# The RMS norms of a hybrid decoder layer: the roots of the rows enter TensorE's turning products as a diagonal matrix

## The chip, the cores and the metric

The kernel runs on one core of one Trainium2 chip. The metric is the device time of one execution in microseconds (us). A profile of one execution lies beside it; its times are counted from the start of its span.

## The reference

One layer of a decoder trunk, float32, 512 tokens behind 16 learned meta tokens, width 2048:

```
def rms_norm(x, g):
    y = x * rsqrt(mean(x * x, axis=-1) + 1e-6)
    return y * g

h = concat(meta_tokens, x)                       # 528 x 2048
proj = rms_norm(h, ln_mix_g) @ w_in              # 528 x 5632
h = h + concat(attention(proj), hgrn2(proj)) @ w_out
h = h[16:]                                       # 512 x 2048
h = h + peer_ffn(rms_norm(h, ln_ffn_g), ...)     # routing, 16384 experts, top 16 of 8 heads
```

Both norms over the width, the one ahead of the input projection and the one ahead of the routing, are what the change touches. The norms over single heads are other code.

## The kernel before, in words

`build` (L2054) calls the stages in order: `norm_rows` for the first norm ("mixnorm", L2150), `project`, `attend`, `recur`, `mix_out`, `norm_rows` for the second norm ("ffnnorm", L2157), `route`, `gate_table`, `experts`. Each stage is a block with a program for each engine, and the engines meet at its end. Nothing is planned by costs: the order on each engine is the order of the code.

`norm_rows` (L112) has the rows in four tiles of 128 tokens by 2048 columns, and in the first norm also 16 meta rows. What follows needs them turned (columns on the partitions), multiplied by a gain that belongs to the column, and split into a high part of type float32r and a low part (the remainder), since products are made of three float32r products (`product`, L341).

- ScalarE (ACT) sums the squares in the first norm (L163), except for one tile that VectorE (DVE) sums (L195); in the second norm the sums come from `mix_out`. ACT takes the square root (L167), then makes the high parts of the first two weight pieces of the next stage (`split_first_high`, L300).
- DVE takes the reciprocal with one correction step (`inverse_root`, L100). It then multiplies each tile by its roots, 128x2048 at a time (L206): in place in the first norm, into the tensor `scaled_rows` in the second. The meta rows follow (L209). Each multiplication raises the semaphore `scaled`.
- TensorE (PE) turns: `turn(tb, c)` (L229) is a transpose of 128 columns c of tile tb, out of the scaled tile with the identity `c_ident` as the other operand, into one of 6 PSUM banks (`NORM_BANKS`); a bank holds column block c of all four tiles. It does columns 0 to 5 of tile 0, then of tiles 1, 2 and 3, waiting for `scaled` before each tile. Then it turns the meta rows (L242, 16 transposes). Then for columns 6 to 15 it waits until the bank is emptied (`low`) and does the four tiles.
- ACT empties each bank into the high part with the gain (L171). DVE then makes the low part out of the same bank (L212) and so frees it. Behind the last column the meta rows are treated likewise (L217, L175, L221).
- GpSimd (POOL) makes the low parts of the two first weight pieces (`split_first_low`, L306, which is L312). In the first norm it narrows a mask ahead of that. In the second it makes `plain_rows` behind that (`plain`, L2137): tile 3 of `scaled_rows` multiplied by the gain as a row, which SyncE (SP) stores (L2135) for the sparse experts. SP waits for POOL there (`plain_ready`); the routing's DVE waits for the store (`plain_stored`, L1569).

Behind the first norm PE begins `project` (L343 to L345, with `w_in`), behind the second `route` (the same lines, with `w_q`; the scores of a head, L1425, are float32 products with the keys, not split).

Of the kernel before, what the change touches and what calls it, by code (L numbers as in the profile page):

```python
# [24 lines left out]
ALU = mybir.AluOpType  # L25
ACT = mybir.ActivationFunctionType
AX = mybir.AxisListType
F32 = mybir.dt.float32
# [4 lines left out]
P = 128  # L33
D = 2048
DC = D // P
T = 512
TB = T // P
M = 16
# [73 lines left out]
def norm_rows(nc, tag, tiles, scaled_tiles, meta, gain, parts, columns, ident, place, kb, stream,  # L112
# [11 lines left out]
    with ExitStack() as ctx:  # L124
        def sem(name):
# [5 lines left out]
        scaled, turned, high, low = sem("scaled"), sem("turned"), sem("high"), sem("low")  # L131
# [3 lines left out]
        stat = place(f"{tag}_stat", [P, 4, 8], F32, kb)  # L135
        squares = [place(f"{tag}_squares{i}", [P, D], F32, kb + 1 + 8 * i) for i in range(2)] \
            if sums is None else []
        meta_whole = place(f"{tag}_meta_whole", [P, DC, M], F32, kb + 17) if meta is not None else None
# [38 lines left out]
        @block.gpsimd  # L177
        def _(pool):
            if pool_first:
                pool_first(pool)  # L180
            stream.split_first_low(pool)
            if pool_last:
                pool_last(pool, scaled)

        @block.vector
        def _(dve):
# [18 lines left out]
            for tb in range(TB):  # L205
                dve.tensor_scalar(scaled_tiles[tb], tiles[tb], stat[:, 3, tb:tb + 1], None, ALU.mult)\  # L206
                    .then_inc(scaled, 1)
            if meta is not None:
                dve.tensor_scalar(meta, meta, stat[0:M, 3, TB:TB + 1], None, ALU.mult).then_inc(scaled, 1)  # L209
# [14 lines left out]
        @block.tensor  # L224
        def _(pe):
            if consts:
                pe.wait_ge(*consts)

            def turn(tb, c):  # L229
                return pe.transpose(banks[c % NORM_BANKS][:, tb, :], scaled_tiles[tb][:, c * P:(c + 1) * P],  # L230
                                    ident[:, :])

            for tb in range(TB):
                pe.wait_ge(scaled, tb + 1)
                for c in range(NORM_BANKS):
                    last = turn(tb, c)
                    if tb == TB - 1:
                        last.then_inc(turned, 1)
            if meta is not None:
                pe.wait_ge(scaled, n)  # L240
                for c in range(DC):
                    last = pe.transpose(meta_bank[:, c, :], meta[:, c * P:(c + 1) * P], ident[0:M, 0:M])  # L242
                last.then_inc(meta_turned, 1)
            for c in range(NORM_BANKS, DC):
                pe.wait_ge(low, c - NORM_BANKS + 1)
                for tb in range(TB):
                    last = turn(tb, c)
                last.then_inc(turned, 1)
# [5 lines left out]
NORM_BANKS = 6  # L254
# [1799 lines left out]
def build(nc, a, out):  # L2054
# [16 lines left out]
    scaled_rows = place("scaled_rows", [P, TB, D], F32, 144)  # L2071
# [20 lines left out]
                                          ("gain_row_in", "plain_ready", "plain_stored"))  # L2092

# [43 lines left out]
    def plain(pool, scaled):  # L2137
        pool.wait_ge(gain_in, 16)
        pool.wait_ge(scaled, TB)
        pool.tensor_tensor(plain_rows[:], scaled_rows[:, TB - 1, :], gain_row[:], ALU.mult).then_inc(plain_ready, 1)  # L2140

    def load_rows(sp, loaded):
        load_early(sp)
        sp.dma_start(meta_rows[:, :], a["meta"]).then_inc(loaded[0], 16)
        for tb in range(TB):
# [4 lines left out]
    spent = norm_rows(nc, "mixnorm", rows, rows, meta_rows[:, :], cst["ln_mix"], hn,  # L2150
                      lambda part, c: part[:, c, M:L].rearrange("p (b t) -> p b t", t=P), cst["ident"],
                      place, 138, w_in, load_rows, (early_in, 16 * len(early)), pool_first=narrow_mask)
# [4 lines left out]
    norm_rows(nc, "ffnnorm", [h[:, tb, :] for tb in range(TB)], [scaled_rows[:, tb, :] for tb in range(TB)],  # L2157
              None, cst["ln_ffn"], xT, lambda part, c: part[:, :, c, :], cst["ident"], place, 136, w_q,
# [78 lines left out]
```

## Time and profile before

| | |
|---|---|
| time, median of 3 runs | 3590.52 us (3590.32 to 3590.65) |
| the profiled execution, its own time | 3590.52 us |
| its span | 3588.7 us |
| PE busy | 3360.4 us (94%) |
| DVE busy | 2234.7 us (62%) |
| ACT busy | 1124.8 us (31%) |
| POOL busy | 1158.9 us (32%) |
| first norm's turning and splitting, from DVE's first scaling to the projection's first product | 19.25 to 38.37 us |
| the same in the second norm, to the routing's first product | 1048.20 to 1069.83 us |

The busy times are sums over the span and overlap each other. PE is TensorE's matmuls, PEld its weight loads. The timeline gives instructions in order of time, merged where they follow each other; in brackets stands how long the engine had been idle and what ended it. Time beyond the span is what lies around the program.

### The profile page before, as it was taken

What the parts mean: (1) busy time and instruction counts of PE and PEld (TensorE: products, weight loads), DVE (VectorE), ACT (ScalarE), POOL (GpSimd) and SP (SyncE); (2) the same over time, 40 slices, a digit from 0 to 9 for tenths busy, and PEclk for the clock granted to TensorE, in tenths of its full rate; (3) what the DMA queues carried; (4) which work ended last, traced back from release to release, by engine and by line L of the source; (5) the groups of instructions that cost most, each with busy time, mean ns of one, the idle gap of its engine ahead of it and who ended that gap; (6) DMA issues with size and microseconds to landing.
All of it is one profiled execution on the core that took longest, in us unless ns stands there. A gap on an engine that the chain in (4) does not pass through costs nothing.

```text
span 3588.7 us, 51464 instructions
## 1 busy us (share of the span) xinstructions
PE 3360.4 (94%) x16926; PEld 2943.4 (82%) x16926; DVE 2234.7 (62%) x3867; ACT 1124.8 (31%) x1743; POOL 1158.9 (32%) x870
## 2 busy tenths in 40 slices
PE   7999999677989957899999999999999999999999
PEld 5778876566868746799899899999998998998998
DVE  2003312695026989677777777767777777777776
ACT  3122223443222239523322222232223233222222
POOL 2344431163435520232332322323333333333322
PEclk9999999798999979999999999999999999999999
DMA  4233320002332204888788888877888887888886
GB/s 139 76 88 94 94 82 15 1 1 101 99 105 83 71 35 187 293 270 267 260 272 265 266 267 267 269 265 261 275 262 265 268 266 261 270 265 265 268 266 232
DMA packets 276020, 686.84 MB, mean 191 GB/s; under 512 B 120544, under 2 KB 120800, under 8 KB 273504
## 3 DMA queue, kind: packets, MB, share of 16 engines
q1 hardware_dynamic: 202224, 417.51, 36.0%
q0 software_dynamic: 73728, 268.47, 22.2%
q8 instruction: 37, 0.61, 0.1%
q14 instruction: 31, 0.25, 0.0%
HBM read 655.48 MB, written 30.41 MB: 191 GB/s over the span
## 4 chain that ended last, share of the span: by engine, by line
PE 59%; ACT 2%; issue 1%; DMA 1%; DVE 0%; ACTq 0%; DVEq 0%; SPq 0%
PE exp_a L1866 10%; PE exp_a L1868 10%; PE exp_a L1867 10%; PE exp_o L1887 10%; PE exp_o L1889 10%; PE exp_o L1885 10%; ACT table_gaps L1684 1%; ACT table_stage L1700 1%; DMA gate_table<-table_stage 0%; PE table_b L1644 0%; DMA exp_raw<-in_v 0%; DVE table_hot L1670 0%; ACTq L1684 0%; ACTq L1700 0%; PE table_t L1635 0%
## 5 line engine op out<-in xcount | busy, mean ns | idle before, releaser
L1866 PE MATMUL exp_a<-x_high,exp_uh 128*128 128x384 f32 x2048 | 685.9, 335 | 11.6 <-DVE exp_ul L1950 11.6
L1868 PE MATMUL exp_a<-x_high,exp_ul 128*128 128x384 f32 x2048 | 685.7, 335 | 0.0
L1867 PE MATMUL exp_a<-x_low,exp_uh 128*128 128x384 f32 x2048 | 685.4, 335 | 0.0
L1889 PE MATMUL exp_o<-exp_vh,exp_al 128*128 128x512 f32 x1536 | 598.2, 389 | 0.0
L1887 PE MATMUL exp_o<-exp_vl,exp_ah 128*128 128x512 f32 x1536 | 598.1, 389 | 0.0
L1885 PE MATMUL exp_o<-exp_vh,exp_ah 128*128 128x512 f32 x1536 | 597.5, 389 | 0.0
L1845 POOL DMA_INDIRECT exp_rows<-in_v_rows,exp_now x256 | 323.6, 1264 | 712.2 <-DVE h L1971 653.7
L1845 POOL DMA_INDIRECT exp_rows<-in_u_rows,exp_now x256 | 298.7, 1167 | 734.2 <-DVE exp_rows L1964 689.2
L1915 ACT CAST exp_vh<-exp_raw 128x1024 fp32r<-128x1024 f32 x256 | 260.1, 1051 | 516.7 <-PE exp_o L1889 493.3
L1950 DVE TENSOR_TENSOR exp_vl<-exp_raw,exp_vh 128x1024 fp32r<-128x1024 f32 x256 | 304.6, 1220 | 166.6 <-ACT exp_vh L1915 165.5
L1866 PEld LDWEIGHTS exp_a<-x_high,exp_uh 128*128 128x128 f32 x2048 | 385.6, 188 | 13.2 <-DVE exp_ul L1950 7.5
L1867 PEld LDWEIGHTS exp_a<-x_low,exp_uh 128*128 128x128 f32 x2048 | 385.5, 188 | 1.2
L1868 PEld LDWEIGHTS exp_a<-x_high,exp_ul 128*128 128x128 f32 x2048 | 385.3, 188 | 0.0
L1926 ACT ACTIVATE exp_act<-exp_a 128x384 f32<-128x384 f32 x128 | 63.0, 492 | 962.5 <-PE exp_a L1868 793.4
L1889 PEld LDWEIGHTS exp_o<-exp_vh,exp_al 128*128 128x128 f32 x1536 | 288.3, 188 | 60.0
L1887 PEld LDWEIGHTS exp_o<-exp_vl,exp_ah 128*128 128x128 f32 x1536 | 288.3, 188 | 59.3
L1885 PEld LDWEIGHTS exp_o<-exp_vh,exp_ah 128*128 128x128 f32 x1536 | 288.3, 188 | 59.2
L1950 DVE TENSOR_TENSOR exp_ul<-exp_raw,exp_uh 128x1024 fp32r<-128x1024 f32 x256 | 309.7, 1221 | 42.0 <-ACT exp_uh L1915 31.6
L312 POOL TENSOR_TENSOR w_in_lo<-w_in_raw,w_in_hi 128x1024 fp32r<-128x1024 f32 x88 | 212.8, 2418 | 333.1 <-ACT w_in_hi L298 333.0
L1971 DVE SCALAR_TENSOR_TENSOR h<-exp_rows,exp_weights,h 128x1024 f32<-128x1024 f32 x256 | 316.5, 1277 | 0.0
L1964 DVE SCALAR_TENSOR_TENSOR exp_rows<-exp_rows,sparse_x 128x1024 f32<-128x1024 f32 x256 | 302.3, 1217 | 0.0
L1991 DVE TENSOR_TENSOR exp_act<-exp_act,exp_gates 128x384 f32<-128x384 f32 x128 | 71.9, 562 | 358.8 <-ACT exp_act L1926 291.5
(292 smaller groups left out, 5194.7 us busy)
## 6 DMA issues: line engine op xcount, KB each, us to landing
exp_raw<-in_u SPq DMA_DIRECT2D x256, 512.0 KB
exp_raw<-in_v SPq DMA_DIRECT2D x256, 512.0 KB
w_in_raw<-in_w_in SPq DMA_DIRECT2D x88, 512.0 KB, 3.6
gate_table<-table_stage SPq DMA_DIRECT2D x6, 4096.0 KB, 11.6
exp_gates<-gate_table SPq DMA_DIRECT2D x128, 192.0 KB
w_out_raw<-in_w_out SPq DMA_DIRECT2D x32, 512.0 KB, 3.6
w_q_raw<-in_w_q SPq DMA_DIRECT2D x32, 512.0 KB, 3.8
x_rows<-in_x SPq DMA_DIRECT2D x4, 1024.0 KB, 8.1
```

Of the source, the lines that this page charges most:

```text
L312: eng.tensor_tensor(self.lo[:, g % 2], self.raw[:, g % RAW], self.hi[:, g % 2].bitcast(F32), ALU.subtract).then_inc(self.low, 1)
L1845: pool.indirect_dma_start(rows[slot][:, :], None, sparse["u" if kind == "dot" else "v"], bass.IndirectOffsetOnAxis(ap=now[:, turn, place_n ...
L1866: pe.matmul(bank, uh[:, b, c, :], xh[:, 0:DENSE_TB, c, :], start=(c == 0), stop=False)
L1867: pe.matmul(bank, uh[:, b, c, :], xl[:, 0:DENSE_TB, c, :], start=False, stop=False)
L1868: last = pe.matmul(bank, ul[:, b, c, :], xh[:, 0:DENSE_TB, c, :], start=False, stop=(c == DC - 1))
L1885: pe.matmul(bank[:, :], ah[:, key, tokens], vh[:, dc % 2, key, :], start=(key == 0), stop=False)
L1887: pe.matmul(bank[:, :], ah[:, key, tokens], vl[:, dc % 2, key, :], start=False, stop=False)
L1889: last = pe.matmul(bank[:, :], al[:, key, tokens], vh[:, dc % 2, key, :], start=False, stop=(key == KEYS_OF_MACRO - 1))
L1915: act.copy(part(uh if split[0] == "u" else vh, *split, half), raw[:, c % RAW_SLOTS, :])\
L1950: dve.tensor_tensor(part(ul if kind == "u" else vl, kind, which, half), raw[:, slot, :], part(uh if kind == "u" else vh, kind, which, half ...
L1964: done = dve.scalar_tensor_tensor(rows[slot][:, :], rows[slot][:, :], 1.0, sparse["x"][:, half, :], ALU.mult, ALU.mult, accum_out=dots[:, ...
L1971: done = dve.scalar_tensor_tensor(sums, rows[slot][:, :], weights[:, pl(pick(m, kind, t), 1)], sums, ALU.mult, ALU.add)
```

## The change

Tiles are no longer multiplied by their roots. DVE instead multiplies the identity by each tile's roots, which gives a 128x128 diagonal matrix (`scales`, one for each tile, and `meta_scale`, 16x16), and PE's transposes become float32 matmuls of the tile with that matrix. `plain`, which had the scaled tile, multiplies tile 3 by its roots on POOL itself, waits for that, and multiplies by the gain row. The tensor `scaled_rows` goes.

```diff
             for tb in range(TB):
-                dve.tensor_scalar(scaled_tiles[tb], tiles[tb], stat[:, 3, tb:tb + 1], None, ALU.mult)\
+                dve.tensor_scalar(scales[:, tb, :], ident[:, :], stat[:, 3, tb:tb + 1], None, ALU.mult)\
                     .then_inc(scaled, 1)
             if meta is not None:
-                dve.tensor_scalar(meta, meta, stat[0:M, 3, TB:TB + 1], None, ALU.mult).then_inc(scaled, 1)
+                dve.tensor_scalar(meta_scale[:, :], ident[0:M, 0:M], stat[0:M, 3, TB:TB + 1], None, ALU.mult)\
+                    .then_inc(scaled, 1)
...
             def turn(tb, c):
-                return pe.transpose(banks[c % NORM_BANKS][:, tb, :], scaled_tiles[tb][:, c * P:(c + 1) * P],
-                                    ident[:, :])
+                return pe.matmul(banks[c % NORM_BANKS][:, tb, :], tiles[tb][:, c * P:(c + 1) * P],
+                                 scales[:, tb, :], start=True, stop=True)
...
                 for c in range(DC):
-                    last = pe.transpose(meta_bank[:, c, :], meta[:, c * P:(c + 1) * P], ident[0:M, 0:M])
+                    last = pe.matmul(meta_bank[:, c, :], meta[:, c * P:(c + 1) * P], meta_scale[:, :],
+                                     start=True, stop=True)
...
-    def plain(pool, scaled):
+    def plain(pool, scaled, roots):
         pool.wait_ge(gain_in, 16)
         pool.wait_ge(scaled, TB)
-        pool.tensor_tensor(plain_rows[:], scaled_rows[:, TB - 1, :], gain_row[:], ALU.mult).then_inc(plain_ready, 1)
+        pool.tensor_scalar(plain_rows[:], h[:, TB - 1, :], roots[:, TB - 1:TB], None, ALU.mult)\
+            .then_inc(plain_scaled, 1)
+        pool.wait_ge(plain_scaled, 1)
+        pool.tensor_tensor(plain_rows[:], plain_rows[:], gain_row[:], ALU.mult).then_inc(plain_ready, 1)
```

## Rows read from the trace of the kernel before

**Rows 1.** The page: busy time, share of the span and instructions of each engine.

```profile
PE 3360.4 (94%) x16926; PEld 2943.4 (82%) x16926; DVE 2234.7 (62%) x3867; ACT 1124.8 (31%) x1743; POOL 1158.9 (32%) x870
```

**Rows 2.** Timeline, first norm: start us, duration us, engine, line, operation [idle before].

```profile
19.25 4.87 DVE L206 TENSOR_SCALAR x_rows<-x_rows,mixnorm_stat 128x2048 f32<-128x2048 f32 x4
...
20.68 4.86 PE L230 MATMUL mixnorm_bank<-c_ident,x_rows 128*128 128x128 f32 x24 [20.68 <-DVE x_rows L206]
...
25.00 9.35 ACT L171 ACTIVATE hn_high<-mixnorm_bank,c_ln_mix 128x512 fp32r<-128x512 f32 x16 [4.94 <-PE mixnorm_bank L230]
25.47 1.07 PEld L242 LDWEIGHTS mixnorm_meta_bank<-c_ident,meta_rows 16*128 16x128 f32 x16 [0.17 <-DVE meta_rows L209]
...
25.72 10.62 DVE L212 SCALAR_TENSOR_TENSOR hn_low<-mixnorm_bank,c_ln_mix,hn_high 128x512 fp32r<-128x512 f32 x16 [0.42 <-ACT hn_high L171]
...
27.18 0.42 PEld L230 LDWEIGHTS mixnorm_bank<-c_ident,x_rows 128*128 128x128 f32 x4 [0.20 <-DVE hn_low L212]
...
38.37 0.79 PE L343 MATMUL proj_bank<-w_in_hi,hn_high 128*128 128x512 f32 x1 [5.27 <-DVEq L484]
```

**Rows 3.** Timeline, second norm, with the same columns.

```profile
1048.17 5.63 POOL L312 TENSOR_TENSOR w_q_lo<-w_q_raw,w_q_hi 128x1024 fp32r<-128x1024 f32 x2 [11.44 <-ACT w_q_hi L304]
1048.20 9.08 DVE L206 TENSOR_SCALAR scaled_rows<-h,ffnnorm_stat 128x2048 f32<-128x2048 f32 x4
...
1051.65 1.54 PE L230 MATMUL ffnnorm_bank<-c_ident,scaled_rows 128*128 128x128 f32 x6 [7.60 <-DVE scaled_rows L206]
...
1057.43 4.55 POOL L2140 TENSOR_TENSOR plain_rows<-scaled_rows,ln_ffn_row 128x2048 f32<-128x2048 f32 x1 [3.62 <-DVE scaled_rows L206]
1058.01 9.36 ACT L171 ACTIVATE x_high<-ffnnorm_bank,c_ln_ffn 128x512 fp32r<-128x512 f32 x16 [8.97 <-PE ffnnorm_bank L230]
1058.73 10.62 DVE L212 SCALAR_TENSOR_TENSOR x_low<-ffnnorm_bank,c_ln_ffn,x_high 128x512 fp32r<-128x512 f32 x16 [1.46 <-ACT x_high L171]
...
1069.83 0.77 PE L343 MATMUL route_q<-x_high,w_q_hi 128*128 128x512 f32 x1 [3.71 <-PEq L124]
```

**Rows 4.** One line's instructions, L206 and L312: duration ns min/median/max, starts us.

```profile
L206 DVE TENSOR_SCALAR x_rows<-x_rows,mixnorm_stat x4: 1280/1281/1286, 19.2 to 22.8; 128x2048 f32<-128x2048 f32 x4
...
L206 DVE TENSOR_SCALAR scaled_rows<-h,ffnnorm_stat x1: 3395/3395/3395, 1048.2 to 1048.2; 128x2048 f32<-128x2048 f32 x1
L312 POOL TENSOR_TENSOR w_q_lo<-w_q_raw,w_q_hi x1: 3327/3327/3327, 1050.5 to 1050.5; 128x1024 fp32r<-128x1024 f32 x1
```

**Rows 5.** Groups by line, gate table, DVE: busy us, mean ns | idle.

```profile
L1670 DVE TENSOR_SCALAR table_hot<-c_iota,picksT 128x128 f32<-128x128 f32 x384 | 103.0, 336 | 0.0
```

**Rows 6.** Float32 products: routing scores, recurrence (timeline), gate table at half clock.

```profile
L1425 PEld LDWEIGHTS route_s<-sub_keys,route_qT x16: 187/192/192, 1098.3 to 1100.1; 128*128 128x128 f32 x16
L1425 PE MATMUL route_s<-sub_keys,route_qT x16: 270/275/275, 1098.5 to 1100.2; 128*128 128x128 f32 x16
...
706.04 1.16 PE L1103 MATMUL rec_g<-rec_halves 128*128 128x128 f32 x8 [1.24 <-DVE rec_halves L1171]
...
L1644 PEld LDWEIGHTS table_b<-table_hot x5: 288/333/338, 1322.1 to 1323.0; 128*128 128x128 f32 x5
```

**Rows 7.** Windows: busy us of each engine, PEclk (granted clock), DMA share, GB/s.

```profile
35.00:36.00 1.00, 0.00 (x0) 0.00 (x0) 1.00 (x3) 0.00 (x0) 0.00 (x0) 0.57 0.00 0
...
41.50:42.00 0.50, 0.50 (x3) 0.38 (x2) 0.00 (x0) 0.00 (x0) 0.00 (x0) 0.54 1.01 410
...
1048.00:1049.00 1.00, 0.00 (x0) 0.00 (x0) 0.96 (x2) 1.00 (x2) 0.83 (x1) 0.95 0.99 418
...
1069.00:1069.80 0.80, 0.00 (x0) 0.00 (x1) 0.36 (x1) 0.00 (x0) 0.00 (x0) 0.73 0.00 0
...
1072.50:1073.00 0.50, 0.50 (x3) 0.43 (x2) 0.00 (x0) 0.00 (x0) 0.00 (x0) 0.71 0.98 385
...
1325.00:1326.00 1.00, 1.00 (x9) 1.00 (x8) 1.00 (x4) 0.15 (x1) 0.00 (x0) 0.81 0.95 348
```

**Rows 8.** Timeline, attention: weight loads of score products with 16 and 256 columns.

```profile
646.36 1.18 PEld L835 LDWEIGHTS att_s<-att_kT,att_qT 128*128 128x128 f32 x8
```

More of the change, by code:

```diff
@@ L106, in inverse_root, with norm_rows @@
     link(dve.tensor_tensor(out, out, spare, ALU.mult))
-def norm_rows(nc, tag, tiles, scaled_tiles, meta, gain, parts, columns, ident, place, kb, stream,
+def norm_rows(nc, tag, tiles, meta, gain, parts, columns, ident, place, kb, scales_kb, stream,
               loads, consts=None, sums=None, pool_first=None, pool_last=None):
@@ L137, in norm_rows @@
             if sums is None else []
+        scales = place(f"{tag}_scales", [P, TB, P], F32, scales_kb)
+        meta_scale = place(f"{tag}_meta_scale", [M, M], F32, kb + 0.25) if meta is not None else None
         meta_whole = place(f"{tag}_meta_whole", [P, DC, M], F32, kb + 17) if meta is not None else None
@@ L182, in _ @@
             if pool_last:
-                pool_last(pool, scaled)
+                pool_last(pool, scaled, stat[:, 3, :])
         @block.vector
@@ L2070, in build @@
     plain_rows = place("plain_rows", [P, D], F32, 185)
-    scaled_rows = place("scaled_rows", [P, TB, D], F32, 144)
     plain_table = nc.dram_tensor("plain_rows_table", [P, D], F32, kind="Internal").ap()
@@ L2092, in build @@
                                           ("gain_row_in", "plain_ready", "plain_stored"))
+    plain_scaled = nc.alloc_semaphore("plain_scaled")
     cst, kb = {}, 193.0
@@ L2149, in build @@
     rows = [x_rows[:, tb, :] for tb in range(TB)]
-    spent = norm_rows(nc, "mixnorm", rows, rows, meta_rows[:, :], cst["ln_mix"], hn,
+    spent = norm_rows(nc, "mixnorm", rows, meta_rows[:, :], cst["ln_mix"], hn,
                       lambda part, c: part[:, c, M:L].rearrange("p (b t) -> p b t", t=P), cst["ident"],
-                      place, 138, w_in, load_rows, (early_in, 16 * len(early)), pool_first=narrow_mask)
+                      place, 138, 164, w_in, load_rows, (early_in, 16 * len(early)), pool_first=narrow_mask)
     spent = project(nc, place, 176.5, w_in, hn, nat, nat_meta, meta_row, turned, cst, spent)
@@ L2156, in build @@
     mix_out(nc, place, w_out, mix, mixT, h, a["x"], cst, sums, w_q.load_start)
-    norm_rows(nc, "ffnnorm", [h[:, tb, :] for tb in range(TB)], [scaled_rows[:, tb, :] for tb in range(TB)],
-              None, cst["ln_ffn"], xT, lambda part, c: part[:, :, c, :], cst["ident"], place, 136, w_q,
+    norm_rows(nc, "ffnnorm", [h[:, tb, :] for tb in range(TB)], None, cst["ln_ffn"], xT, lambda part, c: part[:, :, c, :], cst["ident"], place, 136, 144, w_q,
               load_keys, sums=sums, pool_last=plain)
```

## The prediction

> **What bounds the kernel now.** I read the page's busy times first, then the stretches around the two calls of `norm_rows` in the timeline, then the clock by windows. TensorE is busy for 94% of the span [rows 1], nearly all of it outside the norms, so what counts is by how much a norm delays the product stage behind it. The reader should see in each norm three phases. First VectorE scales four tiles of rows and TensorE turns the first six columns of each tile. Then ACT and DVE empty a bank each 0.66 us (10.62 us for 16 [rows 2, 3]), with TensorE turning the other ten columns beside them: four transposes take 0.42 us of weight loads [rows 2], so TensorE waits there and DVE sets the pace. Last comes a tail: 2.0 us in the first norm from DVE's last full-width low part (25.72 + 10.62 = 36.34) to TensorE's first product (38.37), and 0.5 us in the second (69.35 to 69.83; I leave off the leading thousand for the second norm from here on). Any shift of that first product is passed on whole, because the stages behind it are TensorE's.
>
> **The scaling that goes.** In the first norm it is 4.87 us of DVE [rows 2], but PE is busy with the 24 first transposes in nearly the same time, 4.86 us from 20.68: only the first tile's 1.28 us lies alone on the path [rows 4]. In the second it is 9.08 us [rows 3], because DVE and POOL exclude each other: the first scaling lasts 3.40 us where one of the first norm is 1.28, and POOL's second split 3.33 of the 5.63 that both take, where the first was 2.3 [rows 3, 4]. POOL's first ran 48.17 to 50.5, DVE's scaling only behind it, POOL's second behind that. The Trainium skill ("SBUF — State Buffer", Who interferes with whom) says that whoever issues first holds the shared ports for its whole instruction and the other blocks fully; the trace agrees with it, with these durations.
>
> **What comes in its place on DVE.** A multiplication of a 128x128 tile. The nearest row is a TENSOR_SCALAR of 128x128 with two operations, 0.336 us [rows 5]. I take 0.30 for one operation; no other value between nothing and 0.34 moves the sum by more than 0.3 us a norm. First norm: the first diagonal is ready at 19.25 + 0.30. PE starts 1.43 after DVE's start today, 0.15 after the 1.28 of a scaling, and so at 19.70 then, 0.98 us earlier. The other four diagonals, the meta rows' among them, need 1.2 us together and never gate PE. Second norm: the first diagonal is asked for at 48.20, waits for POOL until 50.3, is ready at 50.6, and PE starts at 50.75 (51.65 today). The second diagonal probably waits for POOL's second split (50.5 to 52.9) and is ready at 53.2; PE needs until 53.4 for the first tile's six products at 0.44, which hides it. The third and fourth follow by 53.9.
>
> **What comes on TensorE.** This is the main term. A transpose of float32 is one weight load and one matmul; a float32 product of 128x128 is two of each: the routing scores of one head are 8 products and the trace counts 16 [rows 6]. The pieces start (1100.2 - 1098.5)/15 = 0.113 us apart at the full clock there, 0.112 from here on; eight in 1.16 us in the recurrence, less the last one's 0.275, are 0.126. At half clock they start (1323.0 - 1322.1)/4 = 0.22 apart [rows 6]. So a column of four products costs PE 8 x 0.112 = 0.90 us where four transposes were out in 0.42. It passes DVE's 0.66: **the second phase becomes TensorE's**.
>
> **The first norm, step by step.** The clock is at half when PE starts: the first 24 transposes take 4.86 us, 0.20 each, twice what they take later, although the record of the clock has no event there. It rose 3.3 us after PE's start in the table stage, 3.6 in the projection, 3.0 in the routing [rows 2, 3, 6, 7]; I take 3.3. From 19.70 to 23.0 PE issues 15 of the first 48 pieces at 0.22; the other 33 at 0.112 take it to 26.7. Bank 0 is complete with piece 38, at 25.6 + 0.3 = 25.9, so ACT starts 0.9 us later than today's 25.00. The meta rows' 16 transposes took 1.07 us [rows 2]; they become 32 pieces with 16 moving columns. The nearest row is the attention's eight score pieces, four of them with 16 columns and four with 256: their loads start (1.18 - 0.19)/7 = 0.14 apart on average [rows 6, 8], and with 0.22 for the wide ones (twice the columns of 0.112) the narrow are 0.085 or less. So 2.7 us, to 29.4; ends: 0.067, as for the transposes, and 0.112, as for full pieces, 2.1 to 3.6 us. Ten columns at 0.90 end at 38.4. Behind the last come 0.2 of matmul latency, ACT's 0.72 (25.00 to 25.72) and DVE's 0.66 with 0.1 for its semaphore: 40.1 for 36.34: **3.7 us later**. With the bounds (meta pieces, 0.112 or 0.126 a piece, clock 3.0 or 3.6 after the start) it is 3.0 to 6.0.
>
> **The second norm.** PE from 50.75, clock up at 54.05 after 15 pieces, 48 pieces out at 57.75, bank 0 at 56.95 (58.01 today). The seventh column needs DVE's first low part, at 56.95 + 1.5 = 58.45; ten columns end at 67.5, the last low part at 69.2 for 69.35: **0.15 us earlier**, between 1.0 earlier and 1.5 later. The gain ahead of the first bank, 1.1 us, is given back by the slower second phase.
>
> **POOL and SP.** `plain` now starts with a multiplication of 128x2048. POOL has no such row; its two-operand multiplication of that size is 4.55 us [rows 3], the upper end. From 53.9 it then ends at 58.4 at the latest and the second at 63.0 (62.0 today), ahead of 69.2, so I cost it and SP's store behind it at nothing. The cover is 6 us; if it went, the barrier at the block's end would wait for POOL.
>
> **The clock behind the norms.** The second norm ends today with PE idle for 3.71 us; the clock fell 0.5 us before the routing's first product and was back at 72.8, 3.0 us after it [rows 3, 7]: 7 products at 0.43 where 0.23 would do, 1.4 us. Now PE idles only from 67.6 to 69.7. The clock fell 2.0, 3.1 and 4.9 us after PE stopped (idle of 5.27, 3.71 and 7.60 us [rows 2, 3], the fall in each by rows 7), so at 2.0 to 2.1 us it most likely stays: **1.4 us earlier**. Behind the first norm PE idles from 38.5 to 42.1, 3.6 us instead of 5.3, and two of the three falls came sooner: I take no gain there, with 1.5 us as the other end.
>
> **Sum.** 3.7 - 0.15 - 1.4 = +2.2 us. The profiled execution took 3590.52 us with a span of 3588.7, 1.8 us around it, and its time is the median of the three runs. Span 3590.9, time **3592.7 us**. That is 0.06%, below the 0.2% (7.2 us) that I count as distinguishable.
>
> **The rivals.**
> 1. *Products keep the clock up where transposes didn't.* The clock in this trace rose during transposes too, so they count for something, but it fell soonest (2.0 us) behind a stretch of them. Then the projection starts at full clock (1.5 us less) and the first pieces are sooner fast (0.3 us): 3590.9. The Trainium skill ("TensorE: Matmul & The Clock Gate", Part 4: PE-mode transpose) says that transpose mode doesn't count as PE-busy in the same way and full clock doesn't engage for it; taken strictly this trace contradicts it, in degree it would favour this rival. Chance 0.25.
> 2. *The small multiplications don't exclude POOL.* Then the second norm's PE starts at 48.6, everything up to the tenth column comes 2 us sooner: 3590.7. For it: nothing in the rows has this size beside POOL; against: the same operation with 2048 columns was blocked. Chance 0.12.
> 3. *A product costs what a transpose costs.* Then DVE's pace stays; the first norm gains 1.0 us and the second 3: 3586.5. The doubled count of the routing scores speaks against it. Chance 0.03. That the scaling isn't removed at all can't be: the calls pass the unscaled tiles.
> 4. *Slower: the clock doesn't rise in the norms, or falls again between bank waits.* PE's second phase then costs 10 x 8 x 0.22 = 17.6 us for 9.0, in both norms: 8.6 us each, 3609.9; in one of them alone, 3601.3. It decides from the point where the clock is at half as column 6 starts (29.4 and 58.5). Against it: PE is denser than today and today the clock is full there. Chance 0.04.
>
> **How the numbers follow.** The forecast has 0.56 and is the likeliest. Its bounds and rivals 1 and 2 reach from 3589 to 3597; what lies outside is rivals 3, 4 and a mishap, some 0.1. Faster by over 0.2% is under 3583.3: 0.01. Slower by over 0.2% is above 3597.7: rival 4 and the upper tail of the piece price, 0.05. Between: 0.94.
>
> **What would show it.** L206 in the changed profile: eight instructions of 128x128 near 0.3 us, two of them in the second norm long because of POOL. L230: twice the count, and in the second phase PE without idle, DVE's L212 waiting for ACT and ACT for PE, 0.9 us a column. ACT's first in the first norm at 25.9, the projection's first product at 42.1, the routing's at 69.7 plus the 3.7 us of the first norm, with full clock there and half at the projection. Wrong would be: L230's count unchanged, DVE still at 0.66 a column, or the products half as dense.

## The result and the profile after

The changed kernel takes 3599.05 us (median of 13 runs, 3594.34 to 3603.4) where the kernel before takes 3590.52 (median of 13, 3585.89 to 3595.69). The ratio is 1.0022 with a 95% interval of 1.0014 to 1.0031: **slower by 7.9 us** (5.0 to 11.1), outside the stated range of 3589 to 3597. (An execution of this kernel differs from the next by up to 9 us, so single times are weak evidence below, and stages are compared instead.) Its profiled execution took 3598.11 us with a span of 3596.3. TensorE gained instructions, 144 net, and 14.6 us of busy time; DVE lost 7.0 us of busy time [rows 1]:

```profile
PE 3375.0 (94%) x17070; PEld 2963.3 (82%) x17070; DVE 2227.7 (62%) x3867; ACT 1127.8 (31%) x1743; POOL 1165.5 (32%) x871
```

144 is 64 more pieces for each norm's tiles and 16 for the meta rows: each transpose became two.

| stage (from the two profiled executions, us) | before | after | shift |
|---|---|---|---|
| first norm, DVE's first multiplication | 19.25 | 19.22 | 0 |
| projection's first product | 38.37 | 45.97 | +7.6 |
| second norm, DVE's first multiplication | 1048.20 | 1054.97 | +6.8 |
| routing's first product | 1069.83 | 1077.33 | +7.5 |
| gate table's first transpose | 1316.50 | 1323.59 | +7.1 |
| end of the span | 3588.7 | 3596.3 | +7.6 |

All of it is there at the projection's first product. The timeline of the first norm in the changed kernel, with the columns of [rows 2]:

```profile
19.22 0.88 DVE L208 TENSOR_SCALAR mixnorm_scales<-c_ident,mixnorm_stat 128x128 f32<-128x128 f32 x4
19.66 8.32 PE L233 MATMUL mixnorm_bank<-mixnorm_scales,x_rows 128*128 128x128 f32 x48 [19.66 <-DVE mixnorm_scales L208]
26.90 3.57 ACT L173 ACTIVATE hn_high<-mixnorm_bank,c_ln_mix 128x512 fp32r<-128x512 f32 x6 [6.86 <-PE mixnorm_bank L233]
...
27.62 4.04 DVE L215 SCALAR_TENSOR_TENSOR hn_low<-mixnorm_bank,c_ln_mix,hn_high 128x512 fp32r<-128x512 f32 x6 [7.39 <-ACT hn_high L173]
27.91 3.74 PE L245 MATMUL mixnorm_meta_bank<-mixnorm_meta_scale,meta_rows 16*128 16x16 f32 x32
...
31.58 10.82 PE L233 MATMUL mixnorm_bank<-mixnorm_scales,x_rows 128*128 128x128 f32 x80
...
34.86 0.69 ACT L173 ACTIVATE hn_high<-mixnorm_bank,c_ln_mix 128x512 fp32r<-128x512 f32 x1 [1.02 <-PE mixnorm_bank L233]
...
38.87 0.69 ACT L173 ACTIVATE hn_high<-mixnorm_bank,c_ln_mix 128x512 fp32r<-128x512 f32 x1 [0.21 <-PE mixnorm_bank L233]
...
45.97 0.79 PE L347 MATMUL proj_bank<-w_in_hi,hn_high 128*128 128x512 f32 x1 [3.57 <-DVEq L488]
```

Before, ACT and DVE each went through sixteen banks in one merged row without a pause [rows 2]. Now they stop after six, and ACT waits for TensorE ahead of each of the other ten: 2.69 us ahead of the first of them, behind the meta pieces, up to 1.02 in the slow stretch, and 0.21 where the clock is full. TensorE has no pause from 19.66 to 42.40 (31.58 + 10.82): the second phase is its own. Yet 80 pieces take 10.82 us there and 9.20 in the second norm, and the windows say why (busy time of PE, PEld, DVE, ACT, POOL, then the granted clock, the DMA share and GB/s):

```profile
31.00:32.00 1.00, 1.00 (x9) 0.97 (x9) 0.66 (x2) 0.00 (x0) 1.00 (x1) 1.00 0.09 16
32.00:33.00 1.00, 1.00 (x8) 1.00 (x7) 0.00 (x0) 0.00 (x0) 0.29 (x1) 0.60 0.00 0
33.00:34.00 1.00, 1.00 (x7) 1.00 (x7) 0.12 (x1) 0.69 (x1) 0.00 (x0) 0.50 0.00 0
34.00:35.00 1.00, 1.00 (x6) 1.00 (x6) 0.63 (x1) 0.14 (x1) 0.00 (x0) 0.50 0.00 0
35.00:36.00 1.00, 1.00 (x9) 1.00 (x8) 0.42 (x1) 0.55 (x1) 0.00 (x0) 0.70 0.00 0
```

PE is busy for the whole of every microsecond, and still the granted clock goes from full (2.4 GHz) to half (1.2 GHz) at about 32.2 and comes back at about 35.6. What TensorE had issued just before the fall are the 32 pieces of the meta rows.

The second norm, timeline, with the columns of [rows 3]:

```profile
1054.95 4.65 POOL L316 TENSOR_TENSOR w_q_lo<-w_q_raw,w_q_hi 128x1024 fp32r<-128x1024 f32 x2 [11.44 <-ACT w_q_hi L308]
1054.97 5.10 DVE L208 TENSOR_SCALAR ffnnorm_scales<-c_ident,ffnnorm_stat 128x128 f32<-128x128 f32 x4
1057.43 8.28 PE L233 MATMUL ffnnorm_bank<-ffnnorm_scales,h 128*128 128x128 f32 x48 [6.60 <-DVE ffnnorm_scales L208]
1060.27 5.44 POOL L2144 TENSOR_SCALAR plain_rows<-h,ffnnorm_stat 128x2048 f32<-128x2048 f32 x1 [0.67 <-DVE ffnnorm_scales L208]
...
1064.62 6.09 ACT L173 ACTIVATE x_high<-ffnnorm_bank,c_ln_ffn 128x512 fp32r<-128x512 f32 x10 [8.81 <-PE ffnnorm_bank L233]
...
1066.15 9.20 PE L233 MATMUL ffnnorm_bank<-ffnnorm_scales,h 128*128 128x128 f32 x80 [0.45 <-DVE x_low L215]
...
1077.33 0.47 PE L347 MATMUL route_q<-x_high,w_q_hi 128*128 128x512 f32 x1 [1.98 <-PEq L124]
```

And L208, one line's instructions (ns min/median/max):

```profile
L208 DVE TENSOR_SCALAR mixnorm_scales<-c_ident,mixnorm_stat x4: 280/280/287, 19.2 to 19.8; 128x128 f32<-128x128 f32 x4
L208 DVE TENSOR_SCALAR ffnnorm_scales<-c_ident,ffnnorm_stat x4: 274/1330/2400, 1055.0 to 1059.8; 128x128 f32<-128x128 f32 x4
```

The multiplication is 0.28 us by itself and 2.40 where POOL had issued first, so POOL's split keeps out the small multiplication too. The four together still take 5.10 us of DVE, but only the first gates TensorE. From DVE's first multiplication to the routing it was 21.63 us and is 22.36.

### The profile page after: what moved, and what is told of

Its sections match the earlier page's. It is cut to its first block, busy times and chain, and to the rows that moved or that the text cites. A ratio compares the mean times of both kernels' runs of the same rounds, so it can differ in the third digit from the quotient of the medians.

```text
span 3596.3 us, 51755 instructions
## 1 busy us (share of the span) xinstructions
PE 3375.0 (94%) x17070; PEld 2963.3 (82%) x17070; DVE 2227.7 (62%) x3867; ACT 1127.8 (31%) x1743; POOL 1165.5 (32%) x871
## 4 chain that ended last, share of the span: by engine, by line
PE 59%; ACT 2%; issue 1%; DMA 1%; ACTq 0%; DVE 0%; DVEq 0%; SPq 0%
PE exp_a L1870 10%; PE exp_a L1872 10%; PE exp_a L1871 10%; PE exp_o L1891 10%; PE exp_o L1893 10%; PE exp_o L1889 10%; ACT table_gaps L1688 1%; ACT table_stage L1704 1%; DMA gate_table<-table_stage 0%; PE table_b L1648 0%; DMA exp_raw<-in_v 0%; ACTq L1688 0%; ACTq L1704 0%; DVE table_hot L1674 0%; PE table_t L1639 0%
## 5 line engine op out<-in xcount | busy, mean ns | idle before, releaser
L1954 DVE TENSOR_TENSOR exp_ul<-exp_raw,exp_uh 128x1024 fp32r<-128x1024 f32 x256 | 309.7, 1220 | 41.9 <-ACT exp_uh L1919 31.6
```

The costliest lines, as they stand in the source:

```text
L1954: dve.tensor_tensor(part(ul if kind == "u" else vl, kind, which, half), raw[:, slot, :], part(uh if kind == "u" else vh, kind, which, half ...
```

## The experiments

### Which norm

The first two runs keep both forms in `norm_rows` and choose by call: products in one norm, scaled rows and transposes as before in the other.

```diff
             for tb in range(TB):
-                dve.tensor_scalar(scales[:, tb, :], ident[:, :], stat[:, 3, tb:tb + 1], None, ALU.mult)\
-                    .then_inc(scaled, 1)
+                dve.tensor_scalar(scales[:, tb, :] if products else scaled_tiles[tb],
+                                  ident[:, :] if products else tiles[tb],
+                                  stat[:, 3, tb:tb + 1], None, ALU.mult).then_inc(scaled, 1)
...
             def turn(tb, c):
+                if not products:
+                    return pe.transpose(banks[c % NORM_BANKS][:, tb, :], scaled_tiles[tb][:, c * P:(c + 1) * P],
+                                        ident[:, :])
```

**Products in the first norm alone.** 

> The change in the first norm alone; the second norm scales its rows and transposes as before. Theory: nearly all of the loss sits in the first norm. The projection's first product at 46.0 us (38.4 before), the stretch from DVE's first scaling to the routing's first product in the second norm 21.6 us as before (1048.20 to 1069.83), time 7.6 us over before. Rival: the loss is spread over later stages (a changed placement in time, not the norms): then the projection starts at 46.0 but the end moves by something else than 7 to 8 us.

Measured: 3598.4 us, ratio 1.0025 (1.0016 to 1.0035): 9.0 us, all of the loss. The timeline's first product of the projection, at 45.46 for 38.37, and the clock's fall in the windows, without a pause of PE:

```profile
45.46 0.79 PE L351 MATMUL proj_bank<-w_in_hi,hn_high 128*128 128x512 f32 x1 [3.57 <-DVEq L492]
```
```profile
31.00:32.00 1.00, 1.00 (x6) 0.97 (x6) 0.15 (x1) 0.00 (x0) 1.00 (x1) 0.55 0.00 0
```

**Products in the second norm alone.** 

> The change in the second norm alone. Theory: the stretch in the second norm is 0.7 us longer (22.4 us for 21.6), the routing then starts at full clock and gets 1.4 us back: 0.7 us faster than before, which no timing here separates from no change. Rival: the second norm costs as much as the first, 3 us or more.

Measured: ratio 1.0003 (0.9994 to 1.0012), no difference. The stretch is 22.40 us (1047.41 to 1069.81), and the routing runs at the full clock from its start.

```profile
1069.81 0.47 PE L349 MATMUL route_q<-x_high,w_q_hi 128*128 128x512 f32 x1 [1.98 <-PEq L124]
```

What follows: the loss is the first norm's, and the two parts (9.0 and 1.1 us by the middles of their intervals) add up to the whole (7.9) within these intervals. The 0.7 us of gain that was expected of the second norm lies inside its interval too.

### The meta rows and the clock

The first norm differs from the second by the meta rows' pieces, and there alone the clock fell. The six runs below change only them; the table also has the first norms of two runs that come further down. The first three columns of numbers are the durations of merged rows of PE's timeline; "to the projection" is counted from TensorE's first piece to the projection's first product, since DVE's start differs by some tenths (17.69 us in the kernel before). The last column is the time, with that of the kernel before from the same series; all but the first two are single executions. Until its first fall the record of the clock shows 1.00 in every trace, also where weight loads of 333 ns show the half clock, so rises in this norm are read from the weight loads.

| run | first 48 | meta pieces | last 80 | clock fell, was back | to the projection | time (before) |
|---|---|---|---|---|---|---|
| after | 8.32 | 3.74 | 10.82 | 32.2, 35.6 | 26.31 | 3599.05 (3590.52) |
| products in the first norm alone | 7.78 | 3.74 | 10.83 | 31.1, 34.5 | 25.77 | 3598.40 (3590.43) |
| after, POOL waits in the second norm | 8.02 | 3.74 | 10.82 | 31.6, 35.0 | 25.99 | 3589.86 (3586.43) |
| scaled rows and products | 7.08 | 4.36 | 11.79 | 30.4, 37.3 | 26.62 | 3599.99 (3586.43) |
| meta rows transposed (16) | 7.00 | 1.17 | 9.20 | not in the norm's pieces | 20.77 | 3594.99 (3590.43) |
| 16 rows, 128 columns | 6.93 | 4.69 | 11.55 | 29.3, 36.1 | 26.58 | 3598.82 (3590.43) |
| 128 rows, 16 columns | 7.27 | 3.90 | 10.56 | 30.1, 33.5 | 24.94 | 3603.05 (3586.43) |
| meta pieces first | 7.88 | 6.97 | 9.20 | rose only at 31 | 27.97 | 3597.24 (3586.43) |
| meta pieces last | 7.11 | 3.79 | 9.20 | 39.8, behind the 80 | 22.66 | 3595.58 (3589.50) |
| meta pieces spread | 7.94 | spread | spread | not in the norm's pieces | 26.93 | 3597.36 (3591.52) |

**Meta rows scaled and transposed as before**, the tiles turned by products:

```diff
-                    last = pe.matmul(meta_bank[:, c, :], meta[:, c * P:(c + 1) * P], meta_scale[:, :],
-                                     start=True, stop=True)
+                    last = pe.transpose(meta_bank[:, c, :], meta[:, c * P:(c + 1) * P], ident[0:M, 0:M])
```

> The changed kernel, but the 16 meta rows are scaled by their roots on DVE and turned by transposes as before. Theory: the meta rows' pieces cost 3.67 us for 1.1 and, beyond that, the TensorE clock falls behind them (0.60 at 32 to 33 us, half until 35.6), which costs 1.7 us in the last ten columns. Projection's first product at 46.0 - 2.6 - 1.7 = 41.7 us, and no half-clock stretch between the first 48 pieces and column 15. Rival (the clock falls at that time whatever is issued): the last ten columns still take 10.6 us, the projection starts at 43.4.

Measured: the projection at 40.65, 5.3 us sooner than in the changed kernel.

```profile
26.81 1.17 PE L244 MATMUL mixnorm_meta_bank<-c_ident,meta_rows 16*128 16x16 f32 x16
27.91 9.20 PE L232 MATMUL mixnorm_bank<-mixnorm_scales,x_rows 128*128 128x128 f32 x80
...
40.65 0.79 PE L345 MATMUL proj_bank<-w_in_hi,hn_high 128*128 128x512 f32 x1 [3.54 <-DVEq L486]
```
```profile
34.00:35.00 1.00, 1.00 (x11) 1.00 (x11) 0.85 (x2) 0.79 (x2) 0.00 (x0) 1.00 0.00 0
```

The clock holds, and all three terms shrink: the meta pieces by 2.6, the slow stretch by 1.6, and the first 48, which this run doesn't touch, by 1.3. So the last is the clock's own scatter. The projection behind it met that scatter too: by windows its clock was back at 46.7, 6.1 us after its first product, where the changed kernel's was back 3.3 us after. The 16 transposes are also over in 1.1 us; a stretch of transposes as long as 3.7 us wasn't tried, so this run says that the pieces of the meta products let the clock fall, not that transposes would have held it.

**Meta pieces with 128 moving columns** instead of 16, their rows still 16. The 16x16 diagonal becomes the first 16 rows of a 128x128 one, and the bank gets 112 columns more, which nothing reads:

```diff
-                    last = pe.matmul(meta_bank[:, c, :], meta[:, c * P:(c + 1) * P], meta_scale[:, :],
+                    last = pe.matmul(meta_bank[:, c * M:c * M + P], meta[:, c * P:(c + 1) * P], meta_scale[:, :],
```

> The changed kernel, but each product of the meta rows has 128 moving columns (16 of the diagonal, 112 zeros, which the next product overwrites) where it had 16; same number of pieces. Theory: the clock falls because pieces with 16 moving columns leave the array idle for most of their 0.112 us although the profile calls TensorE busy. With 128 columns the pieces come at the same 0.112 us, but the clock stays at full: the last ten columns in 9.0 us for 10.6, projection at 44.3. Rival 1 (a contraction over 16 rows, or zeros, is what doesn't count): clock falls as before, 46.0. Rival 2 (wide pieces are dearer): meta stretch over 4 us.

Measured: the clock fell all the same, sooner and for longer (29.3 to 36.1). The theory that narrow columns alone do it falls.

```profile
26.48 4.69 PE L246 MATMUL mixnorm_meta_bank<-mixnorm_meta_scale,meta_rows 16*128 16x128 f32 x32
31.10 11.55 PE L234 MATMUL mixnorm_bank<-mixnorm_scales,x_rows 128*128 128x128 f32 x80
```
```profile
29.00:30.00 1.00, 1.00 (x8) 1.00 (x8) 1.00 (x2) 0.05 (x1) 1.00 (x2) 0.63 0.00 0
```

**Meta pieces with 128 rows and 16 columns** (they read tile 0 and its diagonal, so the meta rows' values are replaced):

```diff
-                    last = pe.matmul(meta_bank[:, c, :], meta[:, c * P:(c + 1) * P], meta_scale[:, :],
+                    last = pe.matmul(meta_bank[:, c, :], tiles[0][:, c * P:(c + 1) * P], scales[:, 0, 0:M],
```

> The changed kernel, but the 32 narrow pieces take their weights from tile 0 of the token rows (128 rows) and 16 columns of its diagonal, instead of 16 rows: the meta rows' values are left out, tokens' values stand in their place. Same count, same 16 moving columns. Theory (what lets the clock fall is a product over 16 of the 128 rows): clock full through 27 to 36 us, last ten columns 9.0 us. Rival (few moving columns or diagonals nearly all zero also let it fall): clock falls 3 to 4 us after the pieces begin, last ten columns over 10 us.

```profile
26.83 3.90 PE L245 MATMUL mixnorm_meta_bank<-mixnorm_scales,x_rows 128*128 128x16 f32 x32
30.56 10.56 PE L233 MATMUL mixnorm_bank<-mixnorm_scales,x_rows 128*128 128x128 f32 x80
```
```profile
30.00:31.00 1.00, 1.00 (x7) 1.00 (x7) 0.68 (x2) 0.00 (x0) 1.00 (x2) 0.53 0.06 16
```

Measured: it fell again. Full rows don't save it either. A piece of 128 rows and 16 columns also starts 3.73/32 = 0.117 us behind the one before (the last half microsecond of them at the half clock), about as a piece of 128 columns does (0.112), so narrow pieces save nothing. What both kinds share is a weight load of 128 columns; that it sets the pace is argued, since no run made it narrower. The run's single time of 3603.05 us (3586.43 beside it) doesn't fit its short first norm; the stretch from the projection to the second norm, which no edit touches, was 1017.3 us in its trace and 1009.8 in that of before.

**Meta pieces ahead of the tiles'**, their diagonal made first by DVE (the block moved above the loop over tiles, and DVE's order turned round):

```diff
+            if meta is not None:
+                pe.wait_ge(scaled, 1)
+                for c in range(DC):
+                    last = pe.matmul(meta_bank[:, c, :], meta[:, c * P:(c + 1) * P], meta_scale[:, :],
+                                     start=True, stop=True)
+                last.then_inc(meta_turned, 1)
             for tb in range(TB):
-                pe.wait_ge(scaled, tb + 1)
+                pe.wait_ge(scaled, tb + 1 + (meta is not None))
```

> The changed kernel with the meta rows' products ahead of the tiles' on TensorE. Theory: products over 16 rows don't raise the clock either: they run at half for all their time, 32 x 0.22 = 7.0 us, and the clock rises only 3 to 6 us after the first 128-row product; projection's first product at 19.3 + 0.4 + 7.0 + 8.3 + 9.0 + 3.5 = 47.5 us or later. Rival (they count as work like any other): the clock rises during them, 3 to 6 us after the first, the 48 first pieces run at full in 5.4 us, projection at 44 us or sooner.

Measured: the projection at 47.53, as the theory said. All 32 ran at the half clock: 6.97 us of issue without a pause and no rise (one line's instructions, ns min/median/max, then the timeline):

```profile
L239 PEld LDWEIGHTS mixnorm_meta_bank<-mixnorm_meta_scale,meta_rows x32: 282/328/328, 19.5 to 26.1; 16*128 16x128 f32 x32
```
```profile
26.46 7.88 PE L233 MATMUL mixnorm_bank<-mixnorm_scales,x_rows 128*128 128x128 f32 x48
34.79 9.20 PE L233 MATMUL mixnorm_bank<-mixnorm_scales,x_rows 128*128 128x128 f32 x80 [0.45 <-DVE hn_low L215]
```

The rise came at about 31, some 4.5 us after the first piece of the tiles and 11.5 after TensorE's first, where full pieces alone saw it after 6.1 us at the latest (below). So the meta pieces neither hold the clock nor bring it up; the second half of this rests on one execution.

**Meta pieces behind the last column** (the same block moved to the end of PE's part):

```diff
                 for tb in range(TB):
                     last = turn(tb, c)
                 last.then_inc(turned, 1)
+            if meta is not None:
+                pe.wait_ge(scaled, n)
+                for c in range(DC):
+                    last = pe.matmul(meta_bank[:, c, :], meta[:, c * P:(c + 1) * P], meta_scale[:, :],
+                                     start=True, stop=True)
+                last.then_inc(meta_turned, 1)
```

> The changed kernel with the meta rows' products behind the tiles' on TensorE. Theory: the clock no longer falls in the first norm's last ten columns (9.2 us for 10.8), the meta pieces lie beside ACT's and DVE's last bank for 1.5 of their 3.7 us: projection's first product at 45.97 - 3.67 - 1.6 + 2.2 = 42.9 us. Rival (the clock falls for another reason): the ten columns still take 10.8 us, projection at 44.5.

```profile
36.30 3.79 PE L250 MATMUL mixnorm_meta_bank<-mixnorm_meta_scale,meta_rows 16*128 16x16 f32 x32
42.27 0.79 PE L347 MATMUL proj_bank<-w_in_hi,hn_high 128*128 128x512 f32 x1 [2.19 <-DVEq L488]
```
```profile
39.00:40.00 1.00, 1.00 (x10) 0.98 (x9) 0.00 (x0) 0.00 (x0) 0.00 (x0) 0.92 0.00 0
```

Measured: the projection at 42.27. The 80 pieces of the columns ran at the full clock throughout, and it fell at 39.8, with the last of the meta pieces being issued, where it cost the norm nothing. It comes 3.7 us sooner than in the changed kernel, second to the transposed meta rows, and still 3.9 later than before.

**Two meta products ahead of each of columns 6 to 13**:

```diff
             for c in range(NORM_BANKS, DC):
                 pe.wait_ge(low, c - NORM_BANKS + 1)
+                if meta is not None and c < DC - 2:
+                    for m in (2 * (c - NORM_BANKS), 2 * (c - NORM_BANKS) + 1):
+                        last = pe.matmul(meta_bank[:, m, :], meta[:, m * P:(m + 1) * P], meta_scale[:, :],
+                                         start=True, stop=True)
```

> The changed kernel with the meta rows' 16 products spread: two of them (0.45 us) ahead of each of columns 6 to 13. Theory: it takes a closed stretch of small products to let the clock fall; between full products they cost their 3.7 us only: clock full from its rise to the end of the first norm, columns and meta pieces together 9.2 + 3.7 = 12.9 us, from 27 to 40, projection at 43.5. Rival (their share of the time is enough, a third here): the clock falls in this stretch too, projection at 45 or later.

```profile
29.61 0.61 PE L248 MATMUL mixnorm_meta_bank<-mixnorm_meta_scale,meta_rows 16*128 16x16 f32 x4
30.16 1.16 PE L233 MATMUL mixnorm_bank<-mixnorm_scales,x_rows 128*128 128x128 f32 x8
31.24 0.61 PE L248 MATMUL mixnorm_meta_bank<-mixnorm_meta_scale,meta_rows 16*128 16x16 f32 x4
...
46.46 0.79 PE L349 MATMUL proj_bank<-w_in_hi,hn_high 128*128 128x512 f32 x1 [3.56 <-DVEq L490]
```

Half right: with full pieces between them the same 32 pieces let the clock stay up (1.00 in every window from the rise to 44), but the time didn't come. A column with its two meta products takes 31.24 - 29.61 = 1.63 us where 0.89 + 4 x 0.115 = 1.35 was due: the eight pieces of a column now take 1.08 of it and the four narrow ones 0.55. Eight times 0.28 is 2.2 us, more than the slow stretch had cost. Why changing between the two kinds costs so much wasn't found.

### Is it the products, or where the scaling is done?

**Rows scaled as before, and turned by products with the identity**:

```diff
-                return pe.transpose(banks[c % NORM_BANKS][:, tb, :], scaled_tiles[tb][:, c * P:(c + 1) * P],
-                                    ident[:, :])
+                return pe.matmul(banks[c % NORM_BANKS][:, tb, :], scaled_tiles[tb][:, c * P:(c + 1) * P],
+                                 ident[:, :], start=True, stop=True)
```

> The kernel before, rows scaled by their roots on DVE, but every transpose replaced by a float32 product with the identity: the price of the products alone. Theory: first norm, TensorE starts at 20.7 and then runs as in the changed kernel, projection at 47.0; second norm, start at 51.65 plus the shift, 48 pieces in 8.2 us from the second tile's 54.9 on or bound by TensorE, stretch 23.5 to 25 us for 21.6. Time 3601. Rival: removing the scaling gave more than 1 us in the first norm, then this one is at 49 or later.

Measured: the projection at 47.13 and 23.31 us for the second norm (1056.60 to 1079.91), where the rows of before give 21.63 and the changed kernel 22.36. So in the second norm the products alone cost 1.7 us. Leaving out the scaling gives back 0.95 between these two executions, which isn't clear of the clock: the same 48 pieces of the second norm took 7.16 to 8.53 us over the executions of the change. In the first norm it is 28.05 us from DVE's start to the projection for 19.12 before and 26.75 in the changed kernel; the clock fell there too, at 30.4, and was back only at 37.3, so its slow stretch was the longer of the two (11.79 us for 10.82). The loss is the products': it is there with the scaling kept.

### The exclusion of POOL

**The kernel before, with POOL waiting for the four scalings in the second norm ahead of its two splits**:

```diff
                 pool_first(pool)
+            if pool_last:
+                pool.wait_ge(scaled, TB)
             stream.split_first_low(pool)
```

> The kernel before with one wait added: in the second norm POOL's first splits wait until DVE has scaled the four tiles. Theory: the 9.08 us of scaling are 4.87 of work and 4.2 of waiting for POOL; with POOL behind it ACT's first full bank comes at DVE's start + 5.7 us for 9.8, the stretch to the routing's first product is 17.5 us for 21.6, the routing still starts at half clock; time 4 us under before. POOL's splits and plain rows end 14.5 us after DVE's start, under cover. Rival: POOL's late splits or its store become the block's end, gain under 1 us.

Measured: ratio 0.9993 (0.9984 to 1.0002), 2.5 us less, which can't be told from no change. The timeline shows what it does:

```profile
1043.52 4.88 DVE L208 TENSOR_SCALAR scaled_rows<-h,ffnnorm_stat 128x2048 f32<-128x2048 f32 x4
...
1060.63 0.47 PE L345 MATMUL route_q<-x_high,w_q_hi 128*128 128x512 f32 x1 [3.71 <-PEq L124]
```

Scaling takes 4.88 us for 9.08 [rows 3], and the stretch 17.11 for 21.63: the exclusion was worth 4.5 us, and one wait on POOL's queue takes it away, whose splits are needed only behind the norm. The Trainium skill ("SBUF — State Buffer", Who interferes with whom) says that issue order decides who blocks; the trace agrees, with these 4.5 us for a change of order alone. Some of that is lost behind it: the routing starts at the full clock but goes to half 1.2 us later (0.50 in 1062 to 1064) and is back at 65, so that its fourteenth product starts 4.64 us behind its first (4.44 before), and from its first product to the gate table it takes 248.0 us for 246.7. That leaves 3.2 us in these two traces, where 4 were expected and the interval's middle is 2.5.

**The changed kernel with the same wait.** 

> The changed kernel, with POOL's first two splits of the second norm waiting for the four diagonals. Theory: POOL's first split is all that holds back the first diagonal (2.40 us for 0.28), so TensorE starts 2.1 us sooner after DVE's first (0.4 for 2.46 us) and the stretch from DVE's first diagonal to the routing's first product is 20.3 us for 22.4. Rival: TensorE is at half clock in that phase and starts its wait for the clock earlier only, gain under 1 us.

```profile
1051.11 0.87 DVE L210 TENSOR_SCALAR ffnnorm_scales<-c_ident,ffnnorm_stat 128x128 f32<-128x128 f32 x4
1051.45 7.25 PE L235 MATMUL ffnnorm_bank<-ffnnorm_scales,h 128*128 128x128 f32 x48 [4.49 <-DVE ffnnorm_scales L210]
```

Measured: 19.23 us (to the routing at 1070.34) for 22.36, 2.1 of them from DVE and POOL and 1.0 from the clock (7.25 us for 8.28). TensorE began so early that the clock hadn't fallen yet: it fell at 1052.2 and was back at 1055.6. Where it lies in another execution is chance: in the next run the same 48 pieces took 7.82. With the exclusion gone from both, products need 19.23 us and scaled rows 17.11.

**Products in the second norm alone, with the wait.** 

> The change in the second norm alone, with the same wait of POOL. Theory: stretch 19.2 us as in the changed kernel with that wait (1051.11 to 1070.34), routing at full clock: 2.4 + 1.4 = 3.8 us under before, no better than the kernel before with the wait. Rival: with the wait the diagonals beat the scaling by more than 1 us.

Measured: 3587.44 us, ratio 0.9990 (0.9981 to 0.9999), with a stretch of 19.79 us (1048.46 to 1068.25) and the routing at the full clock from its start. It is 3.6 us faster than the kernel before by its interval's middle, and its interval overlaps that of the kernel before with the wait. Which of the two is better these runs can't say; both beat the change.

## Why the prediction was wrong

The forecast was +2.2 us and no difference that can be measured; it came to +7.9, an outcome that had a chance of 0.05. The rows of the norms carry the difference, step by step.

- **Right: what bounds the norms.** The pieces doubled, their pace at the full clock is 0.112 us, a column takes 0.893 (0.90 was stated), ACT and DVE wait for TensorE, and the tail behind the last column is 3.57 us of idle PE (3.6 stated). DVE's multiplication is 0.28 (0.30 stated), TensorE starts at 19.66 (19.70 stated).
- **Wrong: "The first norm, step by step"**, the term of 3.7 us, which came to 7.6. Three parts of it were short, 3.8 us together for the 3.9 that were missed. The bounds of 3.0 to 6.0 didn't reach it either; its upper ends add up to about 6.3, not 6.0 (0.9 for the meta pieces, 1.6 for 113 pieces at 0.126, 0.15 for the clock).
  - *The clock's rise.* I took 3.3 us after PE's start, the middle of three rows, with 3.0 to 3.6 as ends. It was 5.6 here: the weight loads fall from 333 to 192 ns at about 25.3, in two overlapping stretches of one line's instructions below. ACT's first bank is at 26.90 where 25.9 was stated, and the 48 pieces are out at 27.91 for 26.7: 1.2 us. The same 48 pieces, issued first, took 6.93 to 8.32 us in eight executions. With 0.22 us a piece ahead of the rise, 0.112 behind it and 0.07 of overlap with the next row that is a rise 3.0 to 5.9 us after PE's start. In the second norm, where the record of the clock has the event, it was back 3.3 to 6.1 us after TensorE's first piece in nine executions with such pieces. Three rows that agree within 0.6 us were no bound. The Trainium skill ("TensorE: Matmul & The Clock Gate", Part 1) says that where the clock rises varies from run to run, with identical kernels seen to issue 6, 11 or 14 slow matmuls; the trace agrees, with a scatter of 2.9 us, and I should have carried it in the range.
  - *The meta pieces.* "0.085 or less" was read out of a mixture of narrow and wide pieces; they came 3.67/32 = 0.115 us apart, at the upper end that I had (0.112): 1.0 us more than the 2.7 taken. The run with 128 rows shows that the number of moving columns doesn't matter (0.117 with 16 there).
  - *The clock behind them.* The step after the meta pieces, "ten columns at 0.90", took the full clock for granted; only the fourth rival had a fall, with a chance of 0.04. It went to half for 3.4 us: 10.82 us for 9.20, or 1.6.

```profile
L233 PEld LDWEIGHTS mixnorm_bank<-mixnorm_scales,x_rows x6: 333/333/333, 23.9 to 24.9; 128*128 128x128 f32 x6
...
L233 PEld LDWEIGHTS mixnorm_bank<-mixnorm_scales,x_rows x9: 192/192/333, 24.7 to 25.9; 128*128 128x128 f32 x9
```

- **The second norm**: -0.15 was stated and +0.73 measured. POOL kept DVE out as stated (TensorE starts 2.46 us behind DVE, 2.55 stated); the 48 pieces took 8.28 us where 7.0 were taken, because the clock was 0.50 through 1060 to 1062 and up only at about 1063, 5.6 us after TensorE's start for 3.3:

```profile
1060.00:1062.00 2.00, 2.00 (x11) 2.00 (x11) 0.07 (x1) 0.00 (x0) 1.73 (x1) 0.50 0.00 0
...
1077.00:1079.00 2.00, 1.67 (x7) 1.42 (x8) 0.00 (x0) 0.00 (x0) 0.00 (x0) 1.00 0.25 49
```

- **The clock behind the norms**: right. PE idles 1.98 us ahead of the routing and the clock stays, second row above. The routing's fourteenth product starts 3.05 us behind its first where it was 4.44: 1.4 us, as stated. At the gate table 0.4 of it is left; that stretch took 243.6 to 246.7 us in the kernels where the routing began and stayed at the full clock, with the same work in it, so the traces don't say where the rest went. Behind the first norm the clock fell and the projection began at half, as stated, but by luck: the windows put the fall at 45.85, 0.12 us ahead of the first product. In three other runs with products (16 rows and 128 columns, meta pieces first, scaled rows and products) the projection began at full and the clock fell 0.1 to 0.8 us later. (The fall behind the second norm of the kernel before, given as 3.1 us after PE's stop, is 3.3 by its row.)
- **POOL**: its multiplication by the roots took 5.44 us, not the 4.55 that I called the upper end; it lay under its cover, as stated.
- **The rivals.** The first, that products keep the clock up where transposes didn't, fell: the clock at the projection was a matter of tenths, as said, and the rise in the second norm was later, not sooner. The second fell with L208's 2.40 us, the third with the doubled count. The fourth had the right mechanism: the clock fell again in the norm's second phase. But it priced a whole second phase at half clock (8.6 us) and blamed the waits between banks. There were none; what lay ahead of the fall were the meta rows' products, and it cost 1.6 us. Its point of decision, "the clock is at half as column 6 starts", missed it by 0.6 us (31.58, the fall at 32.2).

What is shown: 32 products in a row with 16 rows, or 16 columns, or both, let the clock fall in each of seven executions with TensorE busy throughout. 128x128 pieces in a row didn't: the last 80 of the second norm took 9.20 us in all eleven executions that had them. Nor did the narrow ones spread among full ones, in the one execution that had them so. What in the array's activity the clock follows isn't shown.

## What to carry to other kernels

A float32 transpose that becomes a float32 product doubles TensorE's instructions; where the transposes had set no pace, count them at the product's pace (0.89 us a column of four for 0.42) before taking DVE's saving as gain. Price each TensorE stretch at both of its clock's levels, give the rise a scatter of some microseconds, and don't trust a stretch of small matmuls to hold the clock: put it where nothing waits behind it. Ask of two engines that exclude each other which of them is urgent; one wait on the other's queue was worth 4.5 us in its stage here.

## What was not expected of the hardware

- The granted clock fell while TensorE issued without a pause: behind 32 products of 16x16 (32.2, 31.1, 31.6, 30.4 and 39.8 us in five kernels), of 16 rows and 128 columns (29.3), and of 128 rows and 16 columns (30.1). Issued first, such pieces ran 6.9 us without bringing it up.
- A float32 piece with 16 moving columns costs about what one with 128 does: 0.115 to 0.117 us apart, for 0.112.
- Changing between narrow and full pieces cost 0.28 us a column in the one kernel that did it (1.63 us for 1.35, eight times).
- The rise of the clock came 3.0 to 6.1 us after TensorE began, with the same pieces issued in a row.
- POOL's multiplication of 128x2048 by one value a row takes 5.44 us, more than its product of two such tiles, 4.55.
- Executions differ by some microseconds in the stages that no edit touches (the changed kernel's 13 by 9 us in all): from the projection's first product to the second norm it was 1005.4 to 1017.3 us over the profiled executions, with a granted clock in the stretch from 560 to 900 us that differed between them (0.84, 0.84 and 0.80 by three windows in the longest, 0.87, 0.88 and 0.90 in the shortest). An edit worth 2 us is read from its stage, not from single times.
